# Nine weight stages end with a pair of tiles taken by token block; a turn's first-block products stand first; square roots ahead of centring, their table early

## The reference

```python
for i in range(2):
    mix = mlstm_mixer(x, ...) if i == 0 else mla_mixer(x, ...)
    x = layer_norm(DN_ALPHA * x + mix, ln_g[i, 0], ln_b[i, 0])
    x = layer_norm(DN_ALPHA * x + peer_ffn(x, ...), ln_g[i, 1], ln_b[i, 1])
    x = x + jax.nn.sigmoid(x @ ple_w_gate[i]) * (p[i] @ ple_w_proj[i])
# then, once:
x = x + 0.5 * _rms_norm(_swiglu(_rms_norm(x, g1), w_in1, w_out1), h1)
x = x + _rms_norm(_token_mixing(_rms_norm(x, g2), ...), h2)
x = x + 0.5 * _rms_norm(_swiglu(_rms_norm(x, g3), w_in2, w_out2), h3)
```

## Time and profile before

| what | value |
|---|---|
| median of 3 runs | 2645.86 us |
| span of the profiled execution | 2643.4 us |
| PE busy | 2606.3 us (99%) |
| DVE / ACT / POOL busy | 1694.6 / 1484.6 / 641.0 us |
| HBM traffic over the span | 169 GB/s |
| mean granted PE clock (share of full) | 0.998 |

### The profile page before, as it was taken

One profiled execution on the slowest core, in us unless ns is written; L12 is line 12 of the kernel. 1 busy time (PEld: TensorE's weight loads), 2 busy tenths in 40 slices (PEclk: granted clock), 3 DMA queues, 4 the chain that ended last, 5 costly groups with the idle time before them and its releaser, 6 DMA issues.

```text
span 2643.4 us, 42738 instructions
## 1 busy us (share of the span) xinstructions
PE 2606.3 (99%) x14610; PEld 2247.4 (85%) x14610; DVE 1694.6 (64%) x3143; ACT 1484.6 (56%) x2552; POOL 641.0 (24%) x350
## 2 busy tenths in 40 slices
PE   8999999999999999999999999999999999999998
PEld 7789999998888887789999997888888887878887
DVE  4568757885555565459567875555567756555774
ACT  4445578875445454454578875454455545554553
POOL 0007877760000000018877740000001000001000
PEclk9999999999999999999999999999999999999999
DMA  6245544446555554345544446555556555534564
GB/s 221 88 160 175 183 160 144 144 144 205 195 193 191 193 171 141 108 158 178 182 155 142 143 155 206 191 192 194 193 169 202 188 194 168 167 109 162 167 190 153
DMA packets 124320, 447.51 MB, mean 169 GB/s; under 512 B 14312, under 2 KB 14952, under 8 KB 123936
## 3 DMA queue, kind: packets, MB, share of 16 engines
q1 hardware_dynamic: 120096, 434.16, 50.3%
q0 software_dynamic: 2608, 9.08, 1.2%
q10 hardware_dynamic: 1488, 2.59, 0.3%
HBM read 444.74 MB, written 1.05 MB: 169 GB/s over the span
## 4 chain that ended last, share of the span: by engine, by line
PE 94%; DVE 2%; ACT 2%; issue 1%; DMA 0%; ACTq 0%; POOL 0%; DVEq 0%
PE ps L824 42%; PE ps L780 19%; PE ps L785 10%; PE ps L1042 4%; PE ps L796 4%; PE ps L802 4%; PE ps L799 4%; PE ps L1113 1%; PE ps L1013 1%; PE ps L1059 1%; PE ps L731 0%; PE ps L885 0%; ACT w_hi L420 0%; DVE stats L1938 0%; PE ps L1228 0%
## 5 line engine op out<-in xcount | busy, mean ns | idle before, releaser
L420 ACT CAST w_hi<-ring 128x1024 fp32r<-128x1024 f32 (+1 forms) x812 | 851.6, 1049 | 822.0 <-PE ps L824 524.3
L432 DVE TENSOR_TENSOR w_lo<-ring,w_hi 128x1024 fp32r<-128x1024 f32 (+1 forms) x633 | 772.9, 1221 | 555.5 <-ACT w_hi L420 545.9
L432 POOL TENSOR_TENSOR w_lo<-ring,w_hi 128x1024 fp32r<-128x1024 f32 (+1 forms) x179 | 429.4, 2399 | 1595.8 <-ACT w_hi L420 1397.3
L824 PE MATMUL ps<-w_hi,x_parts 128*128 128x512 f32 x2976 | 745.1, 391 | 2.9 <-ACT w_hi L420 1.4
L824 PEld LDWEIGHTS ps<-w_hi,x_parts 128*128 128x128 f32 x2976 | 554.3, 188 | 123.6 <-issue 6.4
L780 PE MATMUL ps<-x_parts,w_hi 128*128 128x512 f32 x2208 | 564.4, 397 | 0.1
L780 PEld LDWEIGHTS ps<-x_parts,w_hi 128*128 128x128 f32 x2208 | 396.2, 189 | 71.2 <-ACT w_hi L420 0.3
L824 PE MATMUL ps<-w_lo,x_parts 128*128 128x512 f32 x1488 | 402.7, 389 | 0.3 <-DVE w_lo L432 0.3
L824 PEld LDWEIGHTS ps<-w_lo,x_parts 128*128 128x128 f32 x1488 | 278.2, 188 | 59.4 <-DVE w_lo L432 1.7
L785 PEld LDWEIGHTS ps<-x_parts,w_lo 128*128 128x128 f32 x2208 | 300.9, 190 | 22.8
L785 PE MATMUL ps<-x_parts,w_lo 128*128 128x256 f32 x2208 | 307.5, 282 | 0.0
(11 more groups left out here) (285 smaller groups left out, 2324.4 us busy)
## 6 DMA issues: line engine op xcount, KB each, us to landing
ring<-in_u SPq DMA_DIRECT2D x256, 512.0 KB, 3.3
ring<-in_v SPq DMA_DIRECT2D x256, 512.0 KB, 4.2
ring<-in_ffn_in SPq DMA_DIRECT2D x88, 512.0 KB, 3.6
ring<-in_ffn_out SPq DMA_DIRECT2D x44, 512.0 KB, 3.7
ring<-in_wq SPq DMA_DIRECT2D x32, 512.0 KB, 3.3
ring<-in_ple_gate SPq DMA_DIRECT2D x16, 512.0 KB, 3.3
SC<-in_rows POOLq DMA_DIRECT2D x11, 512.0 KB, 4.9
ring<-in_a_qk SPq DMA_DIRECT2D x8, 512.0 KB, 4.5
```

Source lines behind the costliest of these rows:

```text
L420: nc.scalar.copy(part(w_hi, i)[:, used(name)], tile(i)[:, used(name)]).then_inc(tiles_hi, 1)
L432: eng.tensor_tensor(part(w_lo, i)[:, at], tile(i)[:, at], part(w_hi, i)[:, at], ALU.subtract).then_inc(tiles_low[LOW[n][0]], 1)
L824: mm = nc.tensor.matmul(acc[:, 2 * tb + f, 0:cnt], x[:, k + c, tb * P:(tb + 1) * P], part(w, i)[:, at:at + cnt], start=(first and n == 0 a ...
```

## The change

- `PAIRED` names nine stages: `a_out`, `v0`, `ple_gate0`, `v1`, `ple_gate1`, `ffn1_out`, `ret_out`, `mix_out`, `ffn2_out`. Their last two tiles go as a pair: both tiles for block 0, then both for block 1. The last tile counts as begun with its first product of block 1. In `v` PE waits for the staged parts of the last tile ahead of the pair.
- `turn_normed` runs all products of block 0 before those of block 1.
- `roots_by_block` takes the root of block 0 ahead of both centring steps.
- `sqrt_table()` is added in `v` (after the copy that stages the last tile) and after `b_out`'s last copy.

```diff
-            def split_wide(name, j, xs, k, first, last, turns=0, width=D, per_tile=1, blocks=None):
+            def split_wide(name, j, xs, k, first, last, turns=0, width=D, per_tile=1, blocks=None,
+                           begins=0):
...
-                                    if n == c == tb == f == 0:
+                                    if n == c == f == 0 and tb == begins:
                                         begins_tile(mm)
...
+            def split_pair(name, j, xs, ks):
+                for tb in range(TB):
+                    split_wide(name, j, xs, ks[0], False, False, blocks=((tb,),))
+                    split_wide(name, j + 1, xs, ks[1], False, True, blocks=((tb,),), begins=1)
...
                 for k in range(0, KC, per_tile):
+                    if name in PAIRED and k >= KC - 2:
+                        if k == KC - 2:
+                            if turn:
+                                moved(pe, SLOT[f"turn_{turn}"] + k // 2)
+                            split_pair(name, k, (x_hi, x_lo), (k, k + 1))
+                        continue
...
-                for f in range(2):
-                    for tb in range(TB):
-                        if f == 0:
-                            pe.wait_ge(diag_ready, TB * DIAG[name] + tb + 1)
+                for tb in range(TB):
+                    pe.wait_ge(diag_ready, TB * DIAG[name] + tb + 1)
+                    for f in range(2):
...
-                for j in range(EXPERT_TILES - BODY, EXPERT_TILES):
+                for j in range(EXPERT_TILES - BODY, EXPERT_TILES - 2):
                     down(j)
+                pe.wait_ge(staged, EXPERT_TILES * (layer + 1))
+                split_pair(f"v{layer}", EXPERT_TILES - 2, (x_hi, x_lo), (BODY - 2, BODY - 1))
...
-                for j in range(FF_TILES):
+                for j in range(FF_TILES - 2):
                     pe.wait_ge(inner_step, 3 * (FF_TILES * (n - 1) + j + 1))
-                    split_wide(f"ffn{n}_out", j, (act_hi, act_lo), j, j == 0, j == FF_TILES - 1)
+                    split_wide(f"ffn{n}_out", j, (act_hi, act_lo), j, j == 0, False)
+                pe.wait_ge(inner_step, 3 * FF_TILES * n)
+                split_pair(f"ffn{n}_out", FF_TILES - 2, (act_hi, act_lo), (FF_TILES - 2, FF_TILES - 1))
...
                 n = LN_TURNS.index(name)
+                square_roots(1, 0)
                 act.wait_ge(mean_ready, n + 1)
                 for f in range(2):
                     at = slice(512 * f, 512 * f + 512)
                     S.activation(X[:, 0, at], X[:, 0, at], ACT.Identity, bias=col[:, 2, 0:1]).then_inc(first_centred, 1)
-                    square_roots(1, f)
+                square_roots(1, 1)
...
                         stage(j + 1)
                     n = j - (EXPERT_TILES - BODY + 2)
+                    if n == 4:
+                        sqrt_table()
...
                 S.copy(x_hi[:, h, :], bank(s)[:, 0:T]).then_inc(mla_out_hi, 1)
+            sqrt_table()
             take_high(act, "wq1", 0)
```

More of the change, by code:

```diff
@@ L103 @@
 DIAG_TURNS = LN_TURNS + ["rms1", "rms2", "rms3"]
+PAIRED = {"a_out", "v0", "ple_gate0", "v1", "ple_gate1", "ffn1_out", "ret_out", "mix_out", "ffn2_out"}
 def starts(items):
```

## The result

| what | before | after |
|---|---|---|
| median of 8 runs, us | 2646.42 (2645.21 to 2648.64) | 2654.61 (2652.65 to 2655.80) |
| ratio, 95% interval | | 1.003 (1.0021 to 1.0040) |
| span of the profiled execution, us | 2643.4 | 2652.7 |

The account below looks back on a forecast made before the run. PE was taken as the bound, busy 99%, with time lost or won only at turns between stages. 9.5 us lost less 2.2 won gives +7.3 on 2645.86, so 2653 us; range 2647.5 to 2657.5.

Parts of the forecast that it names:

- The pair's stall: In stages with a pair, PE waits for the last tile's low part and restarts slowly: 0.70 us, bounds 0.2 to 1.0.
- pairs that hardly stall: Rival: last tile's parts come early enough, PE loses 0.2 per pair and not 0.70; 2648.7 us, chance 0.17.
- The pair in `v`: In v0 and v1 PE also waits for staged parts ahead of the pair, 0.46 more: 1.16 us each.
- The next stage's first cast: At turns behind a pair, ACT's cast waits for a buffer freed later: 1.36 + 0.70 = 2.06 us later.
- the five turns: Turns after ffn1_out, mix_out, ple_gate1 +1.95 each, ple_gate0 +1.66, ret_out +2.0: 9.5 us lost.
- the head start gets through: Rival: first square, sigmoid or sum starts when block 0 is full; five turns win 0.66 each, 2640.4 us, chance 0.06.
- The early table load: In both v, load hidden in ACT's pause to within 0.1 us; rival that it holds ACT longer: 2655.6, chance 0.03.
- The clock: Rival: PE idles about 1.6 us after ffn1_out and mix_out, clock falls, about 3 us each; 2659, chance 0.04.
- The layer norm after `b_out`: No pair there; PE loses its whole wait for the second diagonal: -1.35 us.
- Alone it is worth nothing: Layer norms: root ahead of centring starts centring about 0.2 us later, and by itself changes nothing.
- The total: Whole kernel: 9.5 us lost, 2.2 won, +7.3; median 2653 us, 0.28% slower.

Follow-up runs that it names:

- late_begin: Kernel before, but in both ple_gate, ffn1_out, ret_out and mix_out the last tile counts as begun six products later, without pairs; 2653.0 us, ratio 1.0021.
- pool_waits: Changed kernel with next stage's first cast behind first square or sigmoid, POOL's low part behind POOL's sums or DVE's first sum into X; 2645.4 us, ratio 1.0000.
- low_behind: Changed kernel with roots behind centring, four pairs, next cast behind square or sigmoid, 20 fillers, POOL's low part behind both DVE sums; 2645.7 us, ratio 0.9995.

## Why the prediction was right, step by step

- *The pair's stall*: forecast 0.70. The pair runs from 2184.02 to the fillers' start at 2190.17, 6.15 for 24 products, which unstalled take 5.44: 0.71. What it was worked out from held too: DVE's low part of the last tile starts 1.56 after the first product of the tile ahead in both kernels (2181.20 and 2185.58). The rival of pairs that hardly stall is out.
- *The pair in `v`*: forecast 1.16 in all. PE's bias rows after `v0` start at 982.11 less the 0.66 by which the stage ran late, so 981.45, against 980.16 before: 1.29. The wait ahead of the pair was as forecast (its start 0.45 later, forecast 0.46), and inside the pair the stall was 0.84 (975.83 to 982.11, less 5.44), not 0.70: the forecast left out that PE starts slowly behind that wait as well (four products in 1.19, in the earlier trace rows 1.07). The gains in the layer norm took it up, as forecast: 0.
- *The next stage's first cast*: forecast 2.06 later. `late_begin` shows the 1.36 of it by itself. From this the five turns followed to within 0.06 each, and `late_begin` agrees with the part of them that a later count makes. The rival in which the head start gets through falls with the square at 6.22.
- *The early table load*: hidden. After `b_out` the load began at 1120.49 and the cast behind it at 1121.89, 1.40 later as in the earlier trace rows, and the four layer norms hold no load any more. The rule of the Trainium skill, ScalarE: Activation LUTs, section What ACT_TABLE_LOAD costs, that a drain comes on top, is not borne out: the trace has none in either place; the instruction behind the load starts 0.01 after the load's 1.28.
- *The clock*: with PE idle 1.60 after `ffn1_out` and after `mix_out` it did not fall. Busy time of the first stretch of the changed kernel, with the granted clock behind the last bracket, 1.00, the 2.4 GHz level:

```profile
2193.00:2198.00 5.00, 3.40 (x18) 1.61 (x17) 4.35 (x7) 2.31 (x4) 0.55 (x1) 1.00 0.40 116
```

- *The layer norm after `b_out`*: forecast -1.35, measured -1.02. The step that failed is "Alone it is worth nothing", of the root ahead of centring: it costs 0.2, since DVE's diagonal waits for the end of POOL's scaling. With that PE keeps 0.30 of its wait for the second diagonal, of which the forecast left nothing; with the roots behind 0.09 is left and the same turn wins 1.25. The prediction did not weigh that DVE and POOL get into each other's way; the earlier trace rows would not have shown it, for they hold no row of POOL. But the trace of the kernel before had it in the layer norm after `a_out`, where the same diagonal took 0.70 (at 146.13) and ended 0.08 after POOL's scaling (145.49 to 146.75).
- *The total*: forecast +7.3, turns +7.5, medians +8.2. The 0.7 between is of the size of what the repeats differ by without an edit.

What stays open: why the third tile's transfer lands up to 1.2 us apart in executions of one kernel, and whether a pair would win in the turns after `ffn1_out` and `mix_out` with POOL's low part behind the diagonal too, or on another engine; no run tried that.

## What to carry to other kernels

When a step is taken apart so that its first half is ready earlier, look for what frees the buffers: a count that goes up later holds back the transfer or cast that waits for it, and everything queued behind that on its engine. Ask of each in-order list which waiting instruction stands ahead of the work that was to come earlier; a head start pays only where nothing does, here, as the change left the lists, in the last turn. And try the parts of a change alone: here the parts in the layer norms won 3.3 us by themselves, and the pairs made of that a loss of 7.5.

## What the runs showed of the hardware

- A DVE instruction with two inputs in SBUF waited for the end of a POOL instruction that overlapped it: the sum of 1.23 us took 3.23, 2.01 and 2.02 under POOL's low part, and each ended 1.09 us after that part did (2188.86 and 2187.77, 2190.77 and 2189.68, 2190.21 and 2189.12). That is a full wait, not a slower run: its whole length lies behind POOL's end, less 0.14. The Trainium skill, SBUF — State Buffer, section Who interferes with whom, says that a DVE instruction with two inputs in SBUF, or one in a two-port mode, contends with GpSimd for a port pair that the two engines share, and that this pair is an exclusive lock. The trace agrees, for this sum and for the diagonal of 0.29 us, which took 0.70 to 0.93 under POOL's scaling and 2.40 under its low part; that the diagonal runs in such a mode no run here shows. DVE's scaling with one tensor from PSUM was not held up: 1.28 under POOL's low part (`pool_waits`, 2187.44) as elsewhere.
- The same 2.49 us without work, with the same 20 fillers ahead of it, took TensorE's granted clock down in one turn and not in the other: to 0.50, the 1.2 GHz level, for some 3 us after `mix_out`, while it stayed at 1.00, the 2.4 GHz level, after `ffn1_out` (`low_behind`). With 26 fillers and 1.60 idle it stayed at 1.00 after `ffn1_out` in the changed kernel.
- A transfer's landing can differ by over a microsecond between executions of one kernel (2.17 and 3.33 us of wait at the same tile), so two profiles can differ by this much where the code is the same.
